# A mixture-of-experts tail on Trainium2: one expert block set apart at the end, the other rows gathered and added early

## The reference

```
h = rms_norm(x);  x = x + mixer(h)                      # four branches, gates, output projection
h = rms_norm(x);  x = x + hierarchical_moe(h)
```

```
expert_id, weight = top-1 group of 4, then top-2 of its 4 experts      # 2 experts for each token
a = h @ w1[e];  b = h @ w3[e]                                          # 1024 -> 256
hid = silu(a) * b * weight
out = sum over the two experts of hid @ w2[e]                          # 256 -> 1024
```

## Time and profile before

| | |
|---|---|
| median of three runs | 2073.32 us (2072.55 to 2074.38) |
| profiled execution, span from first to last instruction | 2071.6 us |
| mean granted TensorE clock | 0.983 |
| TensorE busy | 1957.8 us, 95% |
| VectorE busy | 1036.1 us, 50% |
| Activation busy | 529.4 us, 26% |
| GpSimd busy | 379.9 us, 18% |
| DMA | 369.42 MB, mean 178 GB/s |

### The profile page before, as it was taken

One profiled execution on the slowest core, in us unless ns is written; L12 is line 12 of the kernel. 1 busy time (PEld: TensorE's weight loads), 2 busy tenths in 40 slices (PEclk: granted clock), 3 DMA queues, 4 the chain that ended last, 5 costly groups with the idle time before them and its releaser, 6 DMA issues.

```text
span 2071.6 us, 24500 instructions
## 1 busy us (share of the span) xinstructions
PE 1957.8 (95%) x8924; PEld 1259.7 (61%) x8924; DVE 1036.1 (50%) x1854; ACT 529.4 (26%) x1124; POOL 379.9 (18%) x286
## 2 busy tenths in 40 slices
PE   7999999999999998999599999999999999989991
PEld 4555657655656545888355556675555655468871
DVE  3588605554546875111275873354535478541114
ACT  3233312345430011111123332134454200111111
POOL 2322223121120012000233222222122100210003
PEclk9999999999999999999899999999999999999996
DMA  5555658122317405998641211212232292279955
GB/s 220 186 201 211 252 216 325 57 82 92 112 61 289 175 36 208 412 420 308 226 181 41 87 72 56 82 41 77 77 126 87 77 342 82 102 272 423 398 227 193
DMA packets 71781, 369.42 MB, mean 178 GB/s; under 512 B 6080, under 2 KB 8512, under 8 KB 58448
## 3 DMA queue, kind: packets, MB, share of 16 engines
q1 hardware_dynamic: 42656, 278.66, 34.9%
q10 hardware_dynamic: 22096, 64.02, 8.0%
q0 software_dynamic: 6912, 25.17, 3.2%
HBM read 256.63 MB, written 112.25 MB: 178 GB/s over the span
## 4 chain that ended last, share of the span: by engine, by line
PE 83%; DVE 7%; DMA 3%; ACT 3%; issue 2%; POOL 2%; ACTq 0%; DVEq 0%; SPq 0%; POOLq 0%
PE bank L775 35%; PE bank L1688 11%; PE bank L1549 8%; PE bank L1714 5%; PE bank L1574 5%; PE bank L788 4%; PE bank L562 2%; PE bank L753 2%; PE bank L806 2%; PE bank L829 2%; PE bank L885 2%; PE bank L815 2%; DMA blocks<-ring,slots 1%; PE bank L1680 1%; PE bank L870 1%
## 5 line engine op out<-in xcount | busy, mean ns | idle before, releaser
L775 PE MATMUL bank<-hT,ring 128*128 128x384 f32 x1056 | 361.4, 492 | 5.5 <-ACT gbuf L966 5.5
L775 PE MATMUL bank<-x,ring 128*128 128x384 f32 x1056 | 360.7, 490 | 4.0 <-issue 2.6
L775 PEld LDWEIGHTS bank<-hT,ring 128*128 128x128 f32 x1056 | 196.4, 191 | 153.0 <-issue 31.3
L775 PEld LDWEIGHTS bank<-x,ring 128*128 128x128 f32 x1056 | 194.7, 190 | 147.1 <-issue 26.8
L1145 DVE SCALAR_TENSOR_TENSOR reg_a<-cvx,pp,reg_a 128x783 f32<-128x783 f32 x120 | 142.0, 1183 | 4.3
L939 ACT ACTIVATE sums<-bank 128x384 f32<-128x384 f32 x132 | 64.9, 491 | 288.7 <-PE bank L775 286.6
L1106 DVE SCALAR_TENSOR_TENSOR gbuf<-bank,sums 128x384 f32<-128x384 f32 x96 | 53.5, 557 | 137.4 <-PE bank L775 103.7
L2011 DVE SCALAR_TENSOR_TENSOR prob<-prob,bank 128x256 f32<-128x256 f32 x30 | 12.6, 421 | 203.6 <-ACT prob L1783 203.6
L562 PE MATMUL bank<-ring,hT 128*128 128x512 f32 x192 | 88.8, 618 | 1.6 <-ACT hT L581 1.6
L1751 ACT ACTIVATE prob<-x 128x1024 f32<-128x1024 f32 x12 | 12.7, 1057 | 291.7 <-DVE x L1887 291.7
L502 POOL DMA_INDIRECT oT<-blocks,slots x12 | 12.6, 1054 | 392.0 <-DMA blocks<-hT 389.0
(11 more groups left out here) (304 smaller groups left out, 3211.6 us busy)
## 6 DMA issues: line engine op xcount, KB each, us to landing
ring<-in_wd SPq DMA_DIRECT2D x26, 2048.0 KB, 8.5
blocks<-hT SPq DMA_DIRECT2D x16, 3072.0 KB, 20.9
gate_dram<-gbuf ACTq DMA_DIRECT2D x64, 384.0 KB, 2.4
ring<-gate_dram SPq DMA_DIRECT2D x16, 1536.0 KB, 7.8
wide<-in_we SPq DMA_DIRECT2D x8, 2048.0 KB, 16.2
oT<-in_we SPq DMA_DIRECT2D x8, 2048.0 KB, 14.8
reg_b<-in_we SPq DMA_DIRECT2D x8, 2048.0 KB, 14.0
ring<-in_we SPq DMA_DIRECT2D x8, 2048.0 KB, 16.8
```

What stands on the lines that cost most here:

```text
L775: mm = nc.tensor.matmul(bank[i % 2][:, 0:HALF], w[:, k, :], a[:, k, :], start=(k == 0 and r in (0, 1, 3)), stop=(k == 3), skip_group_check ...
```

## The change

`FINAL` is 14. The pipeline runs blocks 0 to 13 (`range(FINAL)`), then comes the loop (expert 15 and further blocks), and then block 14 alone. Block 14's rows are transposed in the pipeline, in step 12. Its up and down come behind the loop on TensorE. Its result goes not to `blocks` but to a DRAM tensor of its own, `final_dram`, of 128 rows and one row of zeros.

The gathers of the two result rows of tiles 0 to 3 are issued by GpSimd as soon as the loop's stores have landed, and DVE adds them at the end of its tail. Tiles 4 and 5 (`EARLY` is 4) are gathered and added in the head, between others. A third gather per tile, from `final_dram`, brings the row of block 14, or zeros where a token has none; DVE adds it with the weight `w_final`. For this the row numbers and weights are split once per layer in block 2 (`split_final`, ten small DVE instructions); a row of block 14 has weight 0 in the first two adds.

Down alternates between banks 4 and 5 and banks 6 and 7 (`y_bank`) and waits for the copy of the block before the last. In the loop and in block 14 the activation is computed in two halves of 128 columns (`up_halves`, `hidden_half`), and down takes the first half before the second is ready. Block 14's two halves of the result are both copied by Activation, and SP stores each as it is ready.

In the head, DVE now computes variance and scale of a tile one right behind the other.

The diff, cut to its core:

```
+FINAL = NE - 2
+FINAL_ROW = P * PER_EXPERT * FINAL
+EARLY = 4
         def y_back(t, c):
             if t == 3:
-                return reg_b[:, 3 * D + c * D:3 * D + (c + 1) * D]
+                return ring[:, 1, c * D:(c + 1) * D]
+        def y_final(t):
+            return reg_b[:, t * D:(t + 1) * D]
+        def gather(pool, layer, t):
+            if t >= 3:
+                pool.wait_ge(gathered[t % 3], gathered_count(layer, t - 3))
+            for c in range(TOP):
...
+        def gather_final(pool, layer, t):
+            if t == 0:
+                pool.wait_ge(final_out, 32 * layer)
+            if t >= 3:
+                pool.wait_ge(final_in[t % 3], final_count(layer, t - 3))
             pool.indirect_dma_start(
+                out=y_final(t), out_offset=None, in_=final_dram,
+                in_offset=bass.IndirectOffsetOnAxis(ap=final_slots[:, t:t + 1], axis=0)).then_inc(final_in[t % 3], 16)
+        def combine(dve, layer, t):
+            dve.wait_ge(gathered[t % 3], gathered_count(layer, t))
+            for c in range(TOP):
+                stt(x[:, t, :], y_back(t, c), w_top[c][:, t:t + 1], x[:, t, :], ALU.mult, ALU.add).then_inc(combined, 1)
+                dve.wait_ge(combined, TOP * T * (layer - 1) + TOP * t + c + 1)
...
         def head_vector(dve, layer):
+            def add_final(t):
+                dve.wait_ge(final_in[t % 3], final_count(layer, t))
+                done(stt(x[:, t, :], y_final(t), w_final[:, t:t + 1], x[:, t, :], ALU.mult, ALU.add), x_new)
...
-                combine(0)
-                variance(0)
-                scale(0)
-                combine(1)
-                variance(1)
-                for t in range(2, T):
-                    combine(t)
-                    scale(t - 1)
-                    if t < T - 1:
-                        variance(t)
+                add_final(0)
+                add_final(1)
+                for t in range(T - 1):
+                    variance(t)
+                    scale(t)
+                    if t + EARLY < T:
+                        combine(dve, layer, t + EARLY)
+                    if t + 2 < T:
+                        add_final(t + 2)
...
         def head_gpsimd(pool, layer):
-            for t in range(T):
-                for c in range(TOP):
-                    gather(pool, t, c)
-                if t == 3:
-                    pool.wait_ge(cleared, layer)
-                    pool.sem_inc(entered, 1)
-                    power(0)
+            gather_final(pool, layer, 0)
+            gather_final(pool, layer, 1)
+            gather(pool, layer, EARLY)
+            gather_final(pool, layer, 2)
+            pool.wait_ge(cleared, layer)
+            pool.sem_inc(entered, 1)
+            gather(pool, layer, EARLY + 1)
+            power(0)
+            for t in range(3, T):
+                gather_final(pool, layer, t)
...
         def tail_sync(sp):
                     sp.wait_ge(more_out, i * 16 + 16)
-                    sp.sem_inc(more_free, 1)
+                    sp.sem_inc(entered, 1)
+                for c in range(2):
+                    sp.wait_ge(y_ev_act, FINAL + c + 1)
+                    sp.dma_start(final_dram[0:P, c * 512:(c + 1) * 512], y_sb[s_fin][:, c * 512:(c + 1) * 512]
+                                 ).then_inc(final_out, 16)
...
         def tail_tensor(pe):
-                for b in range(LAST):
-                    if b + 1 < LAST:
+                for b in range(FINAL):
+                    if b + 1 < FINAL:
                         up(b + 1)
-                    if b + 2 < LAST:
+                    if b + 2 <= FINAL:
                         turn_in(b + 2)
                     down(b)
+                pe.wait_ge(xt_ev, FINAL + 2)
+                pe.wait_ge(hid_done, FINAL)
+                pe.wait_ge(y_ev, FINAL - 1)
+                pe.wait_ge(y_ev_act, FINAL - 1)
                 with pe.Fori(0, trips) as i:
                     pe.wait_ge(more_in, i * 48 + 48)
...
-                    up_products(s_last, t_last).then_inc(more_up, 1)
-                    pe.wait_ge(more_hid, i + 1)
...
+                    for mm in up_halves(s_last, t_last):
+                        mm.then_inc(more_up, 1)
+                    for k in range(2):
+                        pe.wait_ge(more_hid, i * 2 + k + 1)
+                        for c in range(2):
...
+                pe.wait_ge(up_in[t_fin], 16 * (FINAL // SLOTS) + 16)
+                for mm in up_halves(s_fin, t_fin):
+                    mm.then_inc(up_mm, 1)
...
         def tail_scalar(act):
-                    if b == LAST - 2 and layer + 1 < L:
+                    if b == FINAL - 1 and layer + 1 < L:
                         act.dma_start(ring[:, 0, :], wd[(layer + 1) * CHUNKS]).then_inc(head_in[0], 16)
...
+                act.wait_ge(y_out[s_fin], 16 * (FINAL // 2))
+                for c in range(2):
+                    act.wait_ge(down_mm, FINAL + c + 1)
+                    activate(y_sb[s_fin][:, c * 512:(c + 1) * 512], y_bank(FINAL - 1)[c][:, :], ACT.Copy).then_inc(y_ev_act, 1)
         def tail_gpsimd(pool):
...
                 pool.sem_inc(layer_over, 1)
+                for t in range(EARLY):
+                    gather(pool, layer + 1, t)
         def tail_vector(dve):
...
+                for h in range(2):
+                    hidden_half(s_fin, h, th_done, v_exp, hid_done, FINAL + h + 1)
+                dve.sem_inc(layer_over, 1)
+                for t in range(EARLY):
+                    combine(dve, layer + 1, t)
```

More of the change, by code:

```diff
@@ L425, in program @@
         expert_rows = blocks.rearrange("(e t p) d -> e p t d", t=PER_EXPERT, p=P)
-        scattered, scattered_first, gathered = once("scattered"), once("scattered_first"), [once(f"gathered{t}") for t in range(T)]
-        setup_done, stored, gathered_first = once("setup_done"), once("stored"), once("gathered_first")
+        scattered, scattered_first, gathered = once("scattered"), once("scattered_first"), [once(f"gathered{n}") for n in range(T // 2)]
+        setup_done, stored, final_in = once("setup_done"), once("stored"), [once(f"final_in{n}") for n in range(T // 2)]
+        final_out, combined = once("final_out"), once("combined")
         layer_over, cleared, entered = once("layer_over"), once("cleared"), once("entered")
@@ L1461, in tail @@
             below = part(496, SPARE * NE).rearrange("p (j e) -> p j e", j=SPARE)
+            at_final, in_final = (part(752 + 16 * n, T * TOP).rearrange("p (t c) -> p t c", c=TOP) for n in range(2))
+            row_final, w_both = part(784, T), rt[:, 144:144 + TOP * T].rearrange("p (c t) -> p t c", c=TOP)
             start_f, expert_f, block_f = part(704, SPARE), part(720, SPARE + 2), part(736, SPARE + 1)
@@ L1690, in up_products, with up_halves @@
                     return mm
+                def up_halves(s, slot):
+                    for h in range(2):
+                        for n, j in enumerate((h, 2 + h)):
+                            for k in range(KD):
+                                mm = nc.tensor.matmul(bank[s ^ h][:, n * P:(n + 1) * P], up_w[slot][:, k, j * P:(j + 1) * P],
+                                                      xT[s][:, k, :], start=(k == 0), stop=(k == KD - 1))
+                        yield mm
                 def up(b):
@@ L1744, in tail_tensor @@
                     mm.then_inc(more_down, 1)
+                pe.wait_ge(up_in[t_fin], 16 * (FINAL // SLOTS) + 16)
+                for mm in up_halves(s_fin, t_fin):
+                    mm.then_inc(up_mm, 1)
+                pe.wait_ge(down_in[t_fin], 16 * (FINAL // SLOTS) + 16)
+                pe.wait_ge(y_ev, FINAL)
+                pe.wait_ge(y_ev_act, FINAL)
+                for k in range(2):
+                    pe.wait_ge(hid_done, FINAL + k + 1)
+                    for c in range(2):
+                        mm = nc.tensor.matmul(y_bank(FINAL - 1)[c][:, :], hidT[s_fin][:, k, :],
+                                              down_w[t_fin][:, k, c * 512:(c + 1) * 512], start=(k == 0), stop=(k == 1))
+                        if k == 1:
+                            mm.then_inc(down_mm, 1)
             def tail_scalar(act):
@@ L2018, in tail_vector, with split_final, hidden_half @@
                 trips = dve.value_load(table_e[0:1, SPARE + 1:SPARE + 2], min_val=1, max_val=SPARE + 1)
+                def split_final():
+                    done(ts_(at_final, slot_f, float(-FINAL_ROW), None, ALU.add))
+                    done(ts_(in_final, at_final, 0.0, None, ALU.is_ge))
+                    done(stt(in_final, at_final, float(P), in_final, ALU.is_lt, ALU.mult))
+                    done(stt(at_final, at_final, float(-P), in_final, ALU.add, ALU.mult))
+                    done(reduce_(row_final, at_final, AX.X, ALU.add))
+                    done(ts_(row_final, row_final, float(P), None, ALU.add))
+                    done(nc.vector.tensor_copy(final_slots[:, :], row_final), table_done)
```

(11 more changed lines are left out.)

89 lines of the change are left out of this document (46 added, 43 removed).

## The result

The changed kernel takes **2089.16 us** (median of four runs, 2087.18 to 2090.16) against 2073.22 for the kernel before in the same session. The ratio is 1.0075, with a 95% interval of 1.0063 to 1.0087: 15.9 us slower. The forecast was 2079.2 with a range to 2084.0. The direction was right; the size lies 5 us above the range. In what follows one of the eleven executions of e1 (3466.62 us) is in the slow state and out of its ratio, and all others agree within 0.3%.

The account below looks back on a forecast made before the run. TensorE, busy 95% of the span, was taken as the bound, with idle time at the layer ends. Terms 2.7 - 1.2 + 3.0 + 1.4 = +5.9 us on 2073.3 gave 2079.2; range 2072 to 2084.

Parts of the forecast that it names:

- Part 1: Before the looped transposes, TensorE waits for the looped expert's loads: 4.7 us in the first layer, 2.1 in the second.
- M: Time at which TensorE may go on after the looped loads: 989.9 in the first layer, 2005.4 in the second.
- Part 2: From M to the looped down's end: transposes and eviction 2.1 us, products 7.4, down 3.45; M + 13.0.
- Part 3: Early gathers and adds: final block's store lands about D + 15, hidden; x of tile 0 ready at D + 24.3.
- third rival: Final store slow, landing after 7.5 us, not 3: x of tile 0 2.1 us later at each end; 2083.4; chance 0.15.
- Part 4: First layer, x of tile 0 to first transpose: 3.5 us, plus 0.3 for GpSimd; transpose comes 2.7 us later.
- Part 5: Second layer, x of tile 0 to last scale: 24.6 us against 26.1; end 1.2 us earlier.
- Part 6: TensorE's clock falls in the waits before the looped work: +3.0 us in the first layer, +1.4 in the second.
- Part 7: Split of slots and weights in block 2, one more row of zeros, y_back(3) in the ring: no cost.

Follow-up runs that it names:

- e1: The kernel before with only four banks for down and the looped expert's activation in halves; order of blocks, gathers and adds as before: 2068.37 us.
- e2: The changed kernel with SP's parameter load and read of the number of trips ahead of its waits, so the looped loads are issued earlier: 2083.88 us.
- e6: e5 with only tiles 0 and 1 gathered and added early (EARLY = 2), powers between the later tiles' gathers: 2081.3 us.
- e4: The changed kernel with tile 0 scaled before tile 1's final add, and its power ahead of the second gather call, for tile 5: 2086.29 us.
- e8: The changed kernel with 20 useless products of the identity on TensorE in front of the first layer's loop: 2084.55 us.
- e3: The changed kernel with DVE's wait for block 13's store moved behind its copy of the looped transposes: 2083.33 us.
- e5: The changed kernel with the three edits of e2, e3 and e4 together: 2073.66 us.
- e7: e6 with DVE's variance of a tile put between the two adds of the next tile, so its power runs beside an add: 2071.71 us.

## Why the prediction was right in direction and too low

**Part 1, the load wait: right.** Forecast M = 989.9, transposes seen at 989.70, though the idle time is 5.29 instead of 4.7. In the second layer 0.46 us instead of 2.1, since the loads were issued 7.7 us before the end of down of block 12, where 6.8 had been read from before, and landed after 11.6 us instead of 12.3. e2 moved them and the wait went.

**Part 2, "transposes and eviction 2.1 us", failed.** It counted the DVE copy as work and not what stands in front of it on its engine: `dve.wait_ge(y_out[s_last], ...)`. Before, block 13's store had all of block 14's products to land in. With block 14 behind the loop it has nothing. In the second layer the wait is 4.15 us for TensorE, where 0.78 is the copy; in the first it lies behind the load wait, and e2 brings it out. The halves are as forecast: down follows the products without a gap.

**Part 3, "the store lands at about D + 15", failed.** D is the end of the looped down, 1006.10 and 2031.00. Stores issued at D + 10.4 landed 6.3 to 7.9 us later, in the size of the third rival, and the first final gather went out at D + 19.0, not at D + 15.6. x of tile 0 stood at D + 25.2 and D + 25.65 instead of 24.3. The slow store is only a small part of that: DVE, done with tile 3, waited for the first final row 0.18 and 0.27 us. The larger part is the early rows themselves: the sixth gather landed after 7.6 us where 5.6 was taken (that is the second layer's time in the kernel before; its first layer had 7.4), so tile 2's adds began 14.0 us after the first gather instead of 12.6, of which the forecast had 0.7 in hand. That is why the third rival had the store right and its price, 2.1 us at each end, wrong. The slow store is paid for one tile later: the gather of tile 1's final row went out only behind the first one, and its wait of 2.19 and 1.57 us is in part 4. The Trainium skill ("DMA: Bandwidth & Descriptors", "Issuing engines are not separate DMA queues") had said that transfers from different engines interleave on the same 16 DMA engines; that agrees: the looped expert's 512 KB, with nothing beside it, landed after 2.65 us, the last block's 256 KB among eight gathers after 7.1, among four after 4.6 (e6).

**Part 4, "3.5 us" to the transpose and "0.3 us" for GpSimd, failed.** It took 6.35 us (1031.29 to 1037.64): the add of tile 1 was priced as 1.29 us of work, not as a wait for a row that lands 2.19 us later, and the power stands behind seven gathers of which one takes 1.93 us. That is +2.5 us, and +2.2 in the second layer. e4 takes out 2.8 us of it in the first layer and 0.15 us in the second, where the waits behind it take its place.

**Part 5: right from the first scale on** (22.5 us in the second layer), with part 4's miss ahead of it.

**Part 6, the clock: right.** First layer 3.7 us against 3.0, as e8 shows; second layer 9.38 - 7.41 = 2.0 against 1.4, but in the wait for the store, not in the one for the loads. e3 takes the store wait away and the products still take 9.04 us; only with both waits gone (e5) are they at 7.41.

**The sum of what was missed.** First layer: 0.7 up to the looped down, 0.9 more to x of tile 0, 2.5 to the transpose. Second: 1.9 up to the looped down (store wait +3.4, load wait -1.6, the rest the clock and others), 1.35 more to x of tile 0, 2.25 to the last scale. Together 9.6 us, and 2089.2 - 2079.2 is 10.0.

**Part 7, "at nothing": not contradicted.** From the first transpose of the second layer to down of its block 12 it took 971.4 us, before and after (1028.33 to 1999.79, 1037.64 to 2009.05), and the ten small instructions lie within it and beside TensorE. The range was too narrow for two reasons. The wait for block 13's store and the wait for tile 1's final row were put at nothing, without a bound: the first had always been met before, and the second did not exist before. And the slow store, which was a rival with a chance of 0.15, was priced only at tile 0.

## What to carry to other kernels

When a block of work is moved, list what stood in its shadow: every semaphore wait behind it on every engine, with the time at which it is fulfilled now, and not only the wait that the change adds. Work that is hidden behind a store and a gather shares the DMA engines with what it is to hide; here the store behind which the last rows waited landed after 7.1 us beside eight gathers and after 4.6 beside four. Measure the small parts of a combined change alone: here they were the whole gain, 5 us, and the large part took back this and 16 us more. And when an experiment meets its forecast, look into both layers of its trace: e3 met it with half its gain where none was expected.

## What the runs showed of the hardware

What is queued beside a store can weigh more than its size: 2.65 us for 512 KB alone, 6.3 to 7.9 us for 256 KB beside eight indirect gathers, 4.2 to 4.9 beside four.

The clock fell in the wait of 5.3 us of after, and right behind waits of 3.9 us (e2) and 3.5 us (e3), once TensorE worked again. The windows view, first of e2 and then of e3 in both layers, has the granted clock third from the right:

```profile
985.20:989.00 3.80, 0.00 (x0) 0.00 (x0) 0.68 (x1) 0.60 (x1) 0.00 (x0) 0.99 0.84 285
989.00:993.00 4.00, 3.94 (x21) 3.94 (x22) 0.01 (x1) 0.00 (x0) 0.00 (x0) 0.58 0.92 387
```

```profile
984.00:987.50 3.50, 0.00 (x1) 0.00 (x1) 0.69 (x1) 0.60 (x1) 0.00 (x0) 1.00 1.00 389
...
989.00:993.00 4.00, 3.62 (x17) 3.62 (x18) 0.32 (x1) 0.23 (x1) 0.00 (x0) 0.50 0.94 395
...
2012.50:2014.50 2.00, 1.95 (x9) 1.95 (x10) 0.00 (x0) 0.00 (x0) 0.00 (x0) 0.53 0.04 10
```

Products behind single waits of 1.91 us (e8) and 1.55 us (e5) took 7.41 us, the time at full clock. But a short wait is not safe for that: in e3's second layer the clock fell behind waits of 1.25 and 0.78 us (the last row), with 1.09 us of transposes between them, and in e8's second layer products behind 1.28 and 2.30 us took 9.03. What tells these cases from the others is not shown.

GpSimd's power of one column stretches beside DVE's adds. It is shown here in e7 (chain of waits) and in e6 (timeline):

```profile
1028.15 1.15 POOL small L718
```

```profile
1045.02 0.56 POOL L718 TENSOR_TENSOR small<-small 128x1 f32<-128x1 f32 x1 [3.39 <-DVE small L671]
```

It takes 0.56 us while DVE is idle, and 1.15 when it meets an add with two inputs in SBUF (in e7 from 1027.61 to 1028.89). It ends 0.4 us after that add does, and so does another one in e7, which starts at 1040.50, takes 1.52 us and meets an add that ends at 1041.60. The Trainium skill ("GPSIMD Engine Reference", "Specifications") says that GpSimd shares its SBUF interfaces with VectorE and contends with VectorE instructions that have two SBUF inputs; these rows agree. For the indirect gathers the rows do not say as much: one took 1.93 us at 1033.65, beside an add, another 1.02 at 1028.30, also beside adds, and 0.94 is usual.
